# Adding a finished tile's sums to its tokens in two halves, at two places of the next tile

## The chip, the cores and the metric

One core of a Trainium2 chip runs the whole kernel. The metric is the device time of one execution in microseconds (us); lower is better. Engines: PE (TensorE), DVE (VectorE), ACT (ScalarE), POOL (GpSimd), SP (SyncE, which issues loads). On-chip memory is SBUF (the kernel's "arena") and PSUM, eight banks that PE writes.

## The reference, cut to what matters

Two layers of a trunk over 512 latent and 256 context tokens of width 1024. Each has attention, a short and a long convolution, a merge, and then a layer of experts with product keys. The change touches that last part alone:

```python
def chunk(hc):                       # 128 tokens
    q = (hc @ wq).reshape(PEER_CHUNK, PEER_HEADS, 2, PEER_DK // 2)
    s = jnp.einsum('chpd,hpnd->chpn', q, subkeys)
    s1, i1 = lax.top_k(s[:, :, 0], PEER_TOPK)      # 16 of 128
    s2, i2 = lax.top_k(s[:, :, 1], PEER_TOPK)
    ...
    sc, ic = lax.top_k(cand, PEER_TOPK)            # 16 of the 256 sums
    e = ...                                        # expert numbers
    g = jax.nn.softmax(sc, axis=-1)
    a = jax.nn.gelu(jnp.einsum('chkd,cd->chk', u_tab[e], hc))
    return jnp.einsum('chk,chkd->cd', g * a, v_tab[e])
x = x + gt2 * f                                    # f: the chunks' results
```

Each token takes 8 heads x 16 = 128 experts; for each it needs two rows of 1024 numbers, one of `u_tab` and one of `v_tab`. The result of a chunk, times the gate `gt2`, is added to the tokens.

## The kernel before, in words

The class `Experts` works through tiles of 128 tokens: six in the first layer, four in the second. A tile is 8 units (heads) of 16 selections, so 128 selections. For one selection, each of the 128 tokens of the tile has one expert:

- POOL gathers the 128 rows of 2048 numbers (u and v side by side, 1 MB) into one of 8 slots by an indirect DMA (`gather`, L491). It waits for the expert numbers at the start of a unit, and for the slot: `slot_used` must tell that the selection 8 earlier is summed.
- DVE multiplies the u half with the tokens and sums along the row (`dot`, L651): the "dot". It waits for the landing.
- ACT makes the gelu, the weight and a diagonal matrix of it (`weigh`, L504, L508, L515).
- PE multiplies the diagonal with the v half and accumulates in PSUM (`sum_up`, L536). It works in pairs of selections (even, odd): 16 products, of 512 columns each, for a pair, then frees both slots. Even selections put the tokens of each half of the partitions in place, odd ones crosswise.

Two things are put in between on DVE. `dot` steps a generator, `topk`, at k = 3, 5, 7, 9 and 14 of each unit, just after the dot of that k: the five pieces make the 16 experts and the probabilities of the next unit (L549 to L613). And once a tile is summed, its result is added. It lies in four banks of PSUM: half 0 (two banks, 1024 columns) has the products from the upper 64 partitions of the slots, half 1 those from the lower 64. For each half, `add_tile` multiplies two banks with the gates into `junk` (L626) and adds `junk` to the tokens (L629). `junk` is also what the dots write, so all of this is in order on DVE. At the start of a tile, `turn_halves` (L637) makes the crosswise copy of the new tile's tokens for the odd dots.

`add_tile` of a finished tile is called after the second dot of the next one (`SUM_LAG` is 2), or at the end of the last tile. Tiles use the banks in the order (4, 0, 4, 0, 4, 4) in the first layer and (0, 4, 0, 4) in the second (first bank of each). PE waits at the start of a tile for `sum_taken` of the last tile that had the same banks.

The work is spread over phases with barriers. In the first layer a phase with the experts alone (`phase_experts`) goes to 8 dots into the fifth tile (selection 520); the rest of that layer's experts is interleaved with the first stages of the second layer. In the second layer all 512 selections are in one phase of their own. Each phase starts after all engines have finished the one before.

Of the kernel before, what the change touches and what calls it, by code (L numbers as in the profile page):

```python
# [24 lines left out]
ALU = mybir.AluOpType  # L25
# [4 lines left out]
D = 1024  # L30
# [4 lines left out]
NT_LAT, NT_CTX = L_LAT // P, L_CTX // P  # L35
# [363 lines left out]
class Experts:  # L399
# [214 lines left out]
                                ALU.mult).then_inc(self.probs_ready, 1)  # L614
        yield

    def add_tile(self, dve, tile):
        nc, t = self.c.nc, self.tiles[tile]
        x = self.c.xs[:, t]
        dve.wait_ge(self.slot_used, self.per_tile * (tile + 1))  # L620
        dve.wait_ge(self.dotted, self.n_dotted)
        for half in range(2):
            at = self.bank_of(tile, half) * 512
            if half:
                dve.wait_ge(self.x_added, 2 * tile + 1)
            nc.vector.tensor_tensor(self.junk, self.c.psum[:, at:at + D], self.gates[:, t // NT_LAT],  # L626
                                    ALU.mult).then_inc(self.sum_taken, 1)
            dve.wait_ge(self.sum_taken, 2 * tile + half + 1)
            nc.vector.tensor_tensor(x, x, self.junk, ALU.add).then_inc(self.x_added, 1)  # L629
        dve.wait_ge(self.x_added, 2 * tile + 2)  # L630

    def turn_halves(self, dve, tile):
        nc = self.c.nc
# [6 lines left out]
    def dot(self, dve, n):  # L640
        nc = self.c.nc
        for i in range(self.n_dotted, n):
            u, k = divmod(i, TOPK)
            if i % self.per_tile == 0:
                self.turn_halves(dve, i // self.per_tile)
            if k == 0:
                self.parts = self.topk(dve, u + 1) if u + 1 < self.units else iter(())
            if i:
                dve.wait_ge(self.dotted, i)
            dve.wait_ge(self.landed[i % self.ring], 16 * (i // self.ring + 1))  # L650
            nc.vector.scalar_tensor_tensor(out=self.junk, in0=self.slots[i % self.ring][:, 0:D], scalar=1.0,  # L651
                                           in1=self.h2_turned if i % 2 else self.h2N[:, self.tiles[u // PH]],
                                           op0=ALU.mult, op1=ALU.mult, accum_out=self.dots[:, u % 2, k:k + 1]).then_inc(self.dotted, 1)
            self.n_dotted = i + 1
            if k in (3, 5, 7, 9, 14):
                next(self.parts, None)
            tile, j = divmod(self.n_dotted, self.per_tile)
            if tile and j == self.SUM_LAG:
                self.add_tile(dve, tile - 1)
        if n == self.n_all:  # L660
            self.add_tile(dve, len(self.tiles) - 1)


class Share:
# [2175 lines left out]
```

## Time and profile before

| | us |
|---|---|
| median of 3 runs (5434.0 to 5438.31) | 5437.69 |
| profiled execution | 5433.36 |
| its span, first to last instruction | 5431.3 |
| DVE busy | 3330.3 (61%) |
| PE busy | 3760.0 (69%) |
| POOL busy | 2036.3 (37%) |
| ACT busy | 1988.8 (37%) |

The busy shares are means over stages with very different limits; what a change is worth is read from the stage in which it lies. The profile divides the span into 40 slices of 136 us; GB/s is what the DMA engines moved in each. PE's clock can be granted at 2.4 or 1.2 GHz; a granted clock of 0.5 is the lower one, and a mean between 0.5 and 1.0 has both in it.

### The profile page before, as it was taken

The numbers are of one execution on the slowest core, as the hardware profiler recorded it, in microseconds if no ns is written. First come the engines' busy times: TensorE is split into PE (matmuls) and PEld (weight loads), VectorE is DVE, ScalarE is ACT, GpSimd is POOL, SyncE is SP. The second block draws the span as 40 slices with busy tenths as digits, with TensorE's granted clock in tenths as the row PEclk, the third lists the DMA queues.
The fourth block names the chain that finished last, engine by engine and source line by source line (L and its number), as shares of the span: only waits on it lengthen the run. The fifth ranks groups of instructions, "written<-read, shape, count | busy, mean of one in ns | idle before, by whom it ended". The sixth has DMA issues, their size and how long they took to land. (4 is left out here: it accounts for less than half of the span.)

```text
span 5431.3 us, 59703 instructions
## 1 busy us (share of the span) xinstructions
PE 3760.0 (69%) x19504; PEld 1838.0 (34%) x19504; DVE 3330.3 (61%) x7026; ACT 1988.8 (37%) x5136; POOL 2036.3 (37%) x1533
## 2 busy tenths in 40 slices
PE   6899879987565555555577679678976555555554
PEld 3677338876111111111122245246852111111111
DVE  7622452223777777777687777764135777777776
ACT  5432002212443344343354444325223443343443
POOL 5112003212444444444483356211434444444443
PEclk8999989998767777777688889889988777777777
DMA  5012002212999999999998989841327999999998
GB/s 237 16 44 70 4 16 65 63 67 103 400 418 410 416 410 417 415 414 414 378 363 349 367 327 375 349 171 37 98 80 325 421 412 417 413 415 416 411 417 345
DMA packets 230644, 1532.43 MB, mean 282 GB/s; under 512 B 26164, under 2 KB 26740, under 8 KB 58044
## 3 DMA queue, kind: packets, MB, share of 16 engines
q0 software_dynamic: 184320, 1342.26, 60.5%
q1 hardware_dynamic: 46012, 186.36, 9.4%
q8 instruction: 154, 2.52, 0.2%
q14 instruction: 158, 1.29, 0.1%
HBM read 1515.31 MB, written 13.21 MB: 281 GB/s over the span
## 5 line engine op out<-in xcount | busy, mean ns | idle before, releaser
L536 PE MATMUL psum<-arena 64*64 64x512 f32 x10240 | 1769.8, 825 | 1220.8 <-ACT arena L515 1209.6
L491 POOL DMA_INDIRECT arena<-in_uv,arena x1280 | 1462.9, 1143 | 1817.7 <-PE psum L536 1392.6
L651 DVE SCALAR_TENSOR_TENSOR arena<-arena 128x1024 f32<-128x1024 f32 x1280 | 1621.4, 1267 | 697.8 <-DMA arena<-in_uv,arena 653.0
L536 PEld LDWEIGHTS psum<-arena 64*64 64x64 f32 x10240 | 418.1, 169 | 2519.8 <-ACT arena L515 1892.9
L1549 PE MATMUL psum<-view_at,view_at 128*128 128x512 f32 (+1 forms) x4896 | 966.5, 359 | 19.1 <-PEq L165 10.3
L504 ACT ACTIVATE arena<-arena 128x1 f32<-128x1 f32 x1280 | 258.2, 202 | 1850.8 <-DVE arena L651 1811.0
L265 POOL TENSOR_TENSOR view_at<-view_at,view_at 128x1024 fp32r<-128x1024 f32 (+1 forms) x192 | 455.2, 2380 | 1238.7 <-ACT view_at L299 1208.4
L1549 PEld LDWEIGHTS psum<-view_at,view_at 128*128 128x128 f32 x4896 | 815.3, 191 | 185.2 <-issue 54.4
L515 ACT ACTIVATE arena<-arena 128x64 f32<-128x64 f32 x1280 | 445.1, 348 | 52.7 <-PE psum L536 10.9
L508 ACT ACTIVATE arena<-arena 128x1 f32<-128x1 f32 x1280 | 376.9, 294 | 46.7 <-ACT arena L504 0.4
L299 ACT ACTIVATE view_at<-view_at 128x1024 fp32r<-128x1024 f32 (+1 forms) x176 | 163.9, 939 | 330.6 <-DMA view_at<-in_w_in 188.2
L2405 DVE TENSOR_TENSOR view_at<-view_at,psum 128x768 f32<-128x768 f32 (+1 forms) x48 | 39.4, 821 | 376.2 <-PE psum L1549 376.2
L265 DVE TENSOR_TENSOR view_at<-view_at,view_at 128x2048 fp32r<-128x2048 f32 (+5 forms) x106 | 177.0, 1697 | 83.7 <-ACT view_at L2371 37.2
L2468 PE MATMUL psum<-view_at,view_at 128*128 128x512 f32 x480 | 114.5, 402 | 35.2 <-DVE view_at L265 34.1
L1269 PE MATMUL psum<-view_at,view_at 128*128 128x256 f32 (+1 forms) x528 | 96.7, 346 | 28.1 <-PEq L165 28.1
L2468 PEld LDWEIGHTS psum<-view_at,view_at 128*128 128x128 f32 x480 | 93.4, 195 | 56.0 <-issue 34.6
L504 ACT ACT_TABLE_LOAD x85 | 109.1, 1283 | 2.9 <-PEq L165 1.4
L1019 PE MATMUL psum<-view_at,cond 128*4 128x512 f32 x192 | 63.0, 466 | 64.8 <-POOL view_at L265 35.7
L651 DVE DVE_READ_ACCUMULATOR arena<-arena 128x1 f32 x1280 | 104.8, 82 | 0.0
L2240 PE MATMUL psum<-arena 128*128 128x256 f32 (+2 forms) x232 | 80.0, 511 | 34.6 <-DVE arena L2282 34.6
L558 DVE MAX8 arena<-arena 128x8 f32<-128x128 f32 (+1 forms) x240 | 81.5, 339 | 35.9 <-DVE arena L556 1.5
L472 ACT ACT_TABLE_LOAD x80 | 102.6, 1283 | 1.4
(246 smaller groups left out, 3445.6 us busy)
## 6 DMA issues: line engine op xcount, KB each, us to landing
view_at<-in_w_in SPq DMA_DIRECT2D x108, 512.0 KB, 6.6
view_at<-in_w_mod SPq DMA_DIRECT2D x48, 1024.0 KB, 12.9
arena<-in_uv,arena POOLq DMA_INDIRECT x1280
view_at<-in_w_br SPq DMA_DIRECT2D x48, 256.0 KB
view_at<-in_w_out SPq DMA_DIRECT2D x16, 512.0 KB, 8.7
view_at<-in_wq SPq DMA_DIRECT2D x16, 512.0 KB, 3.4
arena<-mod_rows SPq DMA_DIRECT2D x12, 512.0 KB
keep_spectrum<-arena SPq DMA_DIRECT2D x18, 256.0 KB, 6.9
```

The source lines that it names most:

```text
L265: return eng.tensor_tensor(lo, x, hi.bitcast(F32), ALU.subtract)
L299: self._high(act, lambda out, x: self.c.nc.scalar.activation(out, x, ACT.Copy), n)
L472: self.c.nc.scalar.activation(self.exps[:, u % 2], self.topc, ACT.Exp, bias=self.small[:, u % 2, 0:1], accum_out=self.small[:, u % 2, 1:2] ...
L491: nc.gpsimd.indirect_dma_start(out=self.slots[i % self.ring], out_offset=None, in_=self.table, in_offset=bass.IndirectOffsetOnAxis(ap=self ...
L504: nc.scalar.activation(self.gelus[:, q, k:k + 1], self.dots[:, q, k:k + 1], ACT.Gelu).then_inc(self.act_steps, 1)
L508: nc.scalar.activation(self.scaled[:, q, k:k + 1], self.gelus[:, q, k:k + 1], ACT.Copy, scale=self.probs[:, q, k:k + 1]).then_inc(self.act ...
L515: nc.scalar.activation(self.diag[:, i % 4], self.ident2, ACT.Copy, scale=self.scaled[:, q, k:k + 1]).then_inc(self.diag_ready, 1)
L536: last = nc.tensor.matmul(self.c.psum[tokens, at:at + 512], self.diag[rows, k % 4], self.slots[k % self.ring][rows, D + h * 512:D + (h + 1 ...
L651: nc.vector.scalar_tensor_tensor(out=self.junk, in0=self.slots[i % self.ring][:, 0:D], scalar=1.0, in1=self.h2_turned if i % 2 else self.h ...
L1269: last = nc.tensor.matmul(out, h[:, k, at], m[:, lo:hi, k, :], start=(k == 0 and i == 0), stop=(k == KD - 1 and i == 2))
L1549: last = nc.tensor.matmul(c.psum[:, at + lo:at + hi], a[:, k], b[:, k, lo:hi], start=(k == 0 and i == 0), stop=(k == kt - 1 and i == 2))
L2468: last = nc.tensor.matmul(c.bank(2 * (t % 4) + h), a[:, k, t * P:(t + 1) * P], b[:, 4 * h:4 * h + 4, k, :], start=(k == 0 and i == 0), sto ...
```

## The change

The addition of a finished tile is split into its two halves. Where the next tile uses other banks, the first half is added after 5 dots of it and the second after 7; where it uses the same banks, both are added after 2 dots, as before. The last tile of a layer is added at its end, as before.

```diff
-    def add_tile(self, dve, tile):
+    def add_half(self, dve, tile, half):
         nc, t = self.c.nc, self.tiles[tile]
-        x = self.c.xs[:, t]
+        x, at = self.c.xs[:, t], self.bank_of(tile, half) * 512
         dve.wait_ge(self.slot_used, self.per_tile * (tile + 1))
         dve.wait_ge(self.dotted, self.n_dotted)
-        for half in range(2):
-            at = self.bank_of(tile, half) * 512
-            if half:
-                dve.wait_ge(self.x_added, 2 * tile + 1)
-            nc.vector.tensor_tensor(self.junk, self.c.psum[:, at:at + D], self.gates[:, t // NT_LAT],
-                                    ALU.mult).then_inc(self.sum_taken, 1)
-            dve.wait_ge(self.sum_taken, 2 * tile + half + 1)
-            nc.vector.tensor_tensor(x, x, self.junk, ALU.add).then_inc(self.x_added, 1)
-        dve.wait_ge(self.x_added, 2 * tile + 2)
+        if half:
+            dve.wait_ge(self.x_added, 2 * tile + 1)
+        nc.vector.tensor_tensor(self.junk, self.c.psum[:, at:at + D], self.gates[:, t // NT_LAT],
+                                ALU.mult).then_inc(self.sum_taken, 1)
+        dve.wait_ge(self.sum_taken, 2 * tile + half + 1)
+        nc.vector.tensor_tensor(x, x, self.junk, ALU.add).then_inc(self.x_added, 1)
+        dve.wait_ge(self.x_added, 2 * tile + half + 1)
+
+    def add_after(self, tile):
+        same = tile + 1 < len(self.tiles) and self.banks[tile + 1] == self.banks[tile]
+        return (self.SUM_LAG, self.SUM_LAG) if same else (5, 7)
...
             tile, j = divmod(self.n_dotted, self.per_tile)
-            if tile and j == self.SUM_LAG:
-                self.add_tile(dve, tile - 1)
+            for half in range(2):
+                if tile and tile < len(self.tiles) and j == self.add_after(tile - 1)[half]:
+                    self.add_half(dve, tile - 1, half)
         if n == self.n_all:
-            self.add_tile(dve, len(self.tiles) - 1)
+            for half in range(2):
+                self.add_half(dve, len(self.tiles) - 1, half)
```

## Rows read from the trace of the kernel before

**Rows 1.** The page: span; GB/s in 40 slices; the group of the dots.
```profile
span 5431.3 us, 59703 instructions
...
GB/s 237 16 44 70 4 16 65 63 67 103 400 418 410 416 410 417 415 414 414 378 363 349 367 327 375 349 171 37 98 80 325 421 412 417 413 415 416 411 417 345
...
L651 DVE SCALAR_TENSOR_TENSOR arena<-arena 128x1024 f32<-128x1024 f32 x1280 | 1621.4, 1267 | 697.8 <-DMA arena<-in_uv,arena 653.0
```

**Rows 2.** The copies of L637: durations (ns), first and last start.
```profile
L637 DVE COPY arena<-arena x20: 686/689/691, 1354.1 to 5083.8; 64x1024 f32<-64x1024 f32 x20
```

**Rows 3.** Timeline of DVE, undisturbed: start, duration, idle before; eight dots, first and last.
```profile
5385.25 1.22 DVE L651 SCALAR_TENSOR_TENSOR arena<-arena 128x1024 f32<-128x1024 f32 x1 [1.25 <-DMA arena<-in_uv,arena]
...
5402.64 1.23 DVE L651 SCALAR_TENSOR_TENSOR arena<-arena 128x1024 f32<-128x1024 f32 x1 [1.25 <-DMA arena<-in_uv,arena]
```

**Rows 4.** Timeline of DVE, second tile of the second layer: turn, dots 1 to 13.
```profile
4433.52 1.41 DVE L637 COPY arena<-arena 64x1024 f32<-64x1024 f32 x2
...
4437.22 1.23 DVE L651 SCALAR_TENSOR_TENSOR arena<-arena 128x1024 f32<-128x1024 f32 x1 [1.03 <-DMA arena<-in_uv,arena]
...
4438.56 1.22 DVE L626 TENSOR_TENSOR arena<-psum,arena 128x1024 f32<-128x1024 f32 x1
...
4443.59 1.22 DVE L651 SCALAR_TENSOR_TENSOR arena<-arena 128x1024 f32<-128x1024 f32 x1
...
4444.86 1.22 DVE L651 SCALAR_TENSOR_TENSOR arena<-arena 128x1024 f32<-128x1024 f32 x1
...
4448.04 1.23 DVE L651 SCALAR_TENSOR_TENSOR arena<-arena 128x1024 f32<-128x1024 f32 x1
...
4453.76 1.22 DVE L651 SCALAR_TENSOR_TENSOR arena<-arena 128x1024 f32<-128x1024 f32 x1
...
4458.29 1.23 DVE L651 SCALAR_TENSOR_TENSOR arena<-arena 128x1024 f32<-128x1024 f32 x1
...
4459.56 1.22 DVE L651 SCALAR_TENSOR_TENSOR arena<-arena 128x1024 f32<-128x1024 f32 x1
...
4463.95 1.22 DVE L651 SCALAR_TENSOR_TENSOR arena<-arena 128x1024 f32<-128x1024 f32 x1
...
4468.57 1.23 DVE L651 SCALAR_TENSOR_TENSOR arena<-arena 128x1024 f32<-128x1024 f32 x1 [0.85 <-DMA arena<-in_uv,arena]
```

**Rows 5.** Timeline of POOL in the same stretch: gathers of selections 10 and 14.
```profile
4451.62 0.94 POOL L491 DMA_INDIRECT arena<-in_uv,arena  x1 [5.99 <-PE psum L536]
...
4458.78 1.56 POOL L491 DMA_INDIRECT arena<-in_uv,arena  x1 [1.74 <-PE psum L536]
```

**Rows 6.** Timeline of PE in the same stretch: products of two pairs.
```profile
4447.09 3.69 PE L536 MATMUL psum<-arena 64*64 64x512 f32 x16 [5.20 <-ACT arena L515]
4451.54 1.95 PE L536 MATMUL psum<-arena 64*64 64x512 f32 x16 [0.76 <-ACT arena L515]
```

**Rows 7.** Windows: busy us of each engine, granted clock, DMA share, GB/s (last).
```profile
4435.00:4465.00 30.00, 14.66 (x96) 3.41 (x88) 26.80 (x62) 8.45 (x30) 15.36 (x12) 0.77 0.99 392
...
4465.00:4759.70 294.70, 170.40 (x936) 39.73 (x936) 213.33 (x530) 122.89 (x386) 127.92 (x116) 0.72 1.01 415
...
4454.00:4460.00 6.00, 1.95 (x16) 0.51 (x16) 5.35 (x15) 1.89 (x7) 3.65 (x4) 1.00 0.89 306
```

**Rows 8.** Timeline at the end of the first layer's pure stage.
```profile
2672.01 0.15 DVE L578 TENSOR_SCALAR arena<-arena 128x1 f32<-128x1 f32 x1
2672.87 0.33 SPq L954 DMA_DIRECT2D cols<-in_cols  x1
```

**Rows 9.** Timeline: a gather of POOL and the dot of the same selection.
```profile
4676.18 0.94 POOL L491 DMA_INDIRECT arena<-in_uv,arena  x1 [5.34 <-issue]
...
4683.68 1.23 DVE L651 SCALAR_TENSOR_TENSOR arena<-arena 128x1024 f32<-128x1024 f32 x1 [1.29 <-DMA arena<-in_uv,arena]
```

**Rows 10.** Timeline of POOL, then a window: the first gather of the first layer.
```profile
1336.04 1.17 POOL L491 DMA_INDIRECT arena<-in_uv,arena  x1 [4.00 <-DVE arena L601]
...
1337.00:1338.00 1.00, 0.79 (x15) 0.60 (x14) 0.00 (x0) 0.38 (x1) 0.70 (x2) 1.00 0.37 66
```

## The prediction

> **What bounds the kernel now.** I read the page first. The change touches only the expert stage, in which 1280 selections are gathered (1 MB each), dotted with their tokens (L651) and summed. In the slices that hold this stage alone (two stretches of some 1300 us) the core moves 400 to 421 GB/s [rows 1], and nearly all of DVE's idle time before its dots is put down to the landing of a gather. So the stage goes at the pace of its transfers. When nothing disturbs it, a dot starts every 2.485 us: seven steps in 17.39 us [rows 3]. A dot itself takes 1.27 us, so DVE has 1.2 us to spare in each. What DVE does besides costs nothing until it makes DVE so late that the gathers behind it are held up.
>
> How a late dot comes to hold up a transfer: there are eight slots, and the gather of selection m+7 goes into the slot of m-1, which is free once PE has summed the pair (m-1, m). PE waits for ACT's weight, and ACT for the dot of m. Hence the question for every extra microsecond on DVE: how far behind the landings is the *odd* dot of a pair, and how long before its due landing is the next gather issued?
>
> **The transition before.** The timeline of DVE shows one in full [rows 4]. I count selections of the new tile from 0. Dot 1 starts at 4437.22, on waiting for its data; the four operations of the addition run from 4438.56 to 4443.59 (5.03 us), with no wait for PE before them. With dot 1 as time 0, selection j lands at 2.485 (j-1). Dots 2 to 10 start at 6.4, 7.6, 10.8, 12.1, 15.3, 16.5, 21.1, 22.3 and 26.7: the second dot of a pair follows after 1.27, and the pieces of top-k behind dots 3 and 5 take the step to 3.18 us (4444.86 to 4448.04), behind 7 to 4.53, behind 9 to 4.39 [rows 4]. So the lags behind the landings are 3.9, 2.7, 3.4, 2.1, 2.8, 1.6, 3.7, 2.5 and 4.4. DVE has caught up at 4468.57 (dot 13). From dot 1 to there 12 selections took 31.35 us, where 29.82 were due: 1.5 us lost. Not all of that is the addition's: the same transfers lose about as much in places without any addition, since a whole tile lasts 324.8 us, where 128 x 2.485 = 318.1 were due (two tiles lie between the turn at 4433.5 [rows 4] and that of the last tile, whose second copy starts at 5083.8 [rows 2] and the first 0.7 earlier). The windows separate the two better. The 30 us from the start of the tile move 392 GB/s, the other 294.7 us of the tile 415 [rows 7]; over the six full transitions it is 392 to 416, 401 in the mean, against 415. So an addition costs (1 - 401/415) x 30 = 1.0 us of transfer at the most. **This is all that there is to win: six times 1.0 = 6 us, 0.1% of the span.**
>
> **The change part by part.**
>
> *Counts.* Eight tiles are followed by another. In the one case with the same banks (first layer, tile 4 to 5) both halves still come at 2, and the two last tiles of the layers are added as before. Seven transitions change: six inside the pure stage, and tile 3 to 4 of the first layer, which lies right before the end of its phase.
>
> *Instructions.* The same four operations of DVE per tile, none more. The waits on slots and on the last dot are issued twice; before, the first pair of them costs 0.1 us between the end of dot 1 (4437.22 + 1.23) and the addition (4438.56). I take 0.1 us of DVE more per transition, beneath what the rows resolve. The waits on PE are met later than before and were already met then, so they stay free. PE's wait for free banks comes a tile later and is met either way. SP and ACT get nothing new; no DMA issue is added or moved on POOL, but each stands behind the dot that frees its slot.
>
> *Where the work falls.* This is the point. At 2 the addition meets a DVE that is on time, and it has two dots to recover in before top-k starts. At 5 and 7 each half (2.5 us; with its dot the step is 1.34 + 2.52 = 3.86) falls between pieces of top-k, and inside a pair: the first dot of the pair is done, the second, which PE needs, is held back. I run the same recurrence: a dot starts at its landing or when DVE is free. Dots 2 to 11 start at 2.5, 5.0, 8.2, 12.0, 15.2, 19.1, 23.6, 24.9, 29.2 and 30.5, and the lags are 0, 0, 0.7, 2.1, 2.8, 4.1, 6.2, 5.0, 6.9 and 5.7. The odd ones are what counts: before 2.7, 2.1, 1.6, 2.5, 3.2 (dots 3, 5, 7, 9, 11), after 0, 2.1, 4.1, 5.0, 5.7. The change trades one early, modest delay for a later and greater one: from dot 7 on everything is 2.5 us later than before.
>
> *What that does to the gathers.* From the start of an odd dot to the issue of the gather that it frees, the trace has 6.76 us (4444.86 to 4451.62), and 5.02 where PE is quick (4453.76 to 4458.78) [rows 4, 5]. The difference is PE's: 3.69 us for the 16 products of a pair at the granted clock of 1.2 GHz after 5.20 us of idleness, 1.95 at 2.4 GHz [rows 6]. The due landing is 7 x 2.485 = 17.4 us after that of the odd dot. The margin from issue to due landing is thus 17.4 - lag - (5.0 to 6.8). Before, the narrowest is 17.4 - 2.7 - 6.8 = 7.9 us, behind dot 3, and 2 us later the rate falls to 306 GB/s for 6 us [rows 7]. After, it is 6.5 to 8.3 behind dot 7, 5.6 to 7.4 behind 9 and 4.9 to 6.7 behind 11; the slow figures are likelier, since PE now idles 5 us before each of these pairs.
>
> *Its price.* The trace shows no gather with so short a margin in full flow. Upper bound: one issued at 4676.18 was there for its dot at 4683.68, 7.50 us later, and DVE had idled 1.29 us before it, as in the undisturbed beat (1.25) [rows 3, 9]; so 7.5 costs next to nothing; if nothing shorter did, the narrowest margin of 4.9 would cost 2.6 us. Lower bound: the first gather of the stage is issued at 1336.04, and its data begin to move within 2 us (66 GB/s between 1337 and 1338) [rows 10]; with 2.5 us of moving that makes 4.5, less than 4.9, and the loss would be nothing. The middle of the likely margins, 5.5, lies one microsecond above the lower end and two below the upper; I take 0.9. Against it stands what is saved at dot 3, between 0 and 1.0 us; since half of the dip there falls away only to come back later, I take 0.4. Net per transition +0.5 us, from -1.0 to +2.6; six of them **+3.0**.
>
> The Trainium skill ("DMA: Bandwidth & Descriptors", on the anatomy of a gpsimd DMA) gives a DMA issued by gpsimd 2.0 us plus its bytes at 436 GB/s; for 1 MB this is an estimate of 4.4 us. By that rule even the narrowest margin suffices and only the saving is left, so that the six would give -2.4 where my sum has +3.0. The rows here neither confirm nor exclude it, as none that they show goes below 7.5 us.
>
> *The end of the phase.* In the first layer the pure stage ends after 8 dots of tile 4. DVE ends it: its last piece of top-k starts at 2672.01 and the next phase's first load is issued at 2672.87 [rows 8]. That piece stands behind dot 7, which is 2.5 us later after the change (19.1 against 16.5). Every engine meets at this barrier, so nothing hides it: **+2.5**, at least 0 if the next phase's first loads were not what it waits for.
>
> *Sum.* 3.0 + 2.5 = +5.5 us. The profiled execution took 5433.4 us (span 5431.3), which makes 5438.9; against the median of the runs, 5437.7, which lies 4.3 above it, **5443.2 us**.
>
> **The rivals.** A measurement of this kernel tells about 0.2%, 10.9 us, from no change.
> (a) *The ring runs dry* (slower). Each late gather costs the whole upper price: the place is the gathers issued behind dots 7, 9 and 11; 6 x 2.6 + 2.5 = +18.1, 5455.8 us. It decides from (10.9 - 2.5)/6 = 1.4 us net per transition. For it: the narrowest margin falls from 7.9 to as little as 4.9 us, at three gathers in a row, and PE stays at its lower clock. Against it: even 4.9 covers the start and the moving of the first gather's rows [rows 10].
> (b) *The ring holds, and the dip is gone* (a little faster). Six times -1.0, + 2.5 = -3.5, 5434.2 us. For it: the lower bound of the price, and that the early dip has its cause removed. Against it: the later lags are twice the earlier. The rule of the Trainium skill named above points to this case. Still within 0.2%: faster by over 0.2% would need 13 us from the transitions, where only 6 are lost.
> (c) *The change does nothing to the stage*: as DVE is on time again by dot 15, only the barrier moves: +2.5, 5440.2.
>
> **How the numbers follow.** My forecast 0.45, (c) 0.22, (b) 0.17, (a) 0.16. The likeliest is 5443.2. The range reaches from (b) to a little short of (a)'s end: 5434 to 5455. Slower by over 0.2% is (a) less its weaker part, plus a little of the forecast's upper tail: 0.15. Faster by over 0.2%, for something that no row shows: 0.03. Within 0.2%: 0.82.
>
> **What would show it.** In the timeline of DVE around a transition: two operations behind dot 4, two behind dot 6, no wait for PE; dots 2 and 3 on waiting for their data; dot 10 about 29 us after dot 1. On POOL: the gap of 7 us before the gather of selection 10 gone, longer gaps before 14, 16 and 18. In the windows: the dip of transfer moved by some 10 us to later and not smaller. At the end of the first pure phase: the last piece of top-k 2.5 us later relative to the tile's start. I am wrong if the rate in the 45 us behind a transition falls by more than 1.4 us of transfer (a), or if the pace has no dip at all (b).

## The result, and the profile after

The changed kernel takes 5445.63 us (median of 21 runs, 5437.76 to 5452.53), the kernel before in the same 21 rounds 5435.33 (5428.42 to 5443.33). The ratio is 1.0018, 95% interval 1.0012 to 1.0024: slower by some 10 us (6.5 to 13), where I had forecast +5.5 and put the time at 5443.2, range 5434 to 5455. So the forecast held in direction and range, but the loss is nearly twice my sum. The interval lies on both sides of 0.2%, and the estimate itself is below it. In the rounds of the experiments, one execution of e8 (6048.5 us) and one of the kernel before (5561.7) ran at a lower mean granted clock (0.62 and 0.72, where the others have 0.81 to 0.82), and the ratios leave them out. The profiled execution has a span of 5443.3 us against 5431.3; single executions of either kernel differ by 10 us and more, so what follows goes by stretches of the trace and not by spans.

The timeline of DVE at the same place of the changed kernel as [rows 4] (start, duration, kind of operation, idle before). The lines of the dots are now L655, of the addition L625 and L628. The rows are dots 1, 4, the first half, 5, 6, the second half, 7, 8, 10, 13, 19, 20 and 21:

```profile
4444.98 1.23 DVE L655 SCALAR_TENSOR_TENSOR arena<-arena 128x1024 f32<-128x1024 f32 x1 [0.98 <-DMA arena<-in_uv,arena]
...
4453.71 1.22 DVE L655 SCALAR_TENSOR_TENSOR arena<-arena 128x1024 f32<-128x1024 f32 x1
...
4455.05 1.23 DVE L625 TENSOR_TENSOR arena<-psum,arena 128x1024 f32<-128x1024 f32 x1
...
4457.57 1.22 DVE L655 SCALAR_TENSOR_TENSOR arena<-arena 128x1024 f32<-128x1024 f32 x1
...
4460.76 1.22 DVE L655 SCALAR_TENSOR_TENSOR arena<-arena 128x1024 f32<-128x1024 f32 x1
...
4462.09 1.22 DVE L625 TENSOR_TENSOR arena<-psum,arena 128x1024 f32<-128x1024 f32 x1
...
4464.60 1.22 DVE L655 SCALAR_TENSOR_TENSOR arena<-arena 128x1024 f32<-128x1024 f32 x1
...
4469.11 1.23 DVE L655 SCALAR_TENSOR_TENSOR arena<-arena 128x1024 f32<-128x1024 f32 x1
...
4474.77 1.23 DVE L655 SCALAR_TENSOR_TENSOR arena<-arena 128x1024 f32<-128x1024 f32 x1
...
4478.57 1.22 DVE L655 SCALAR_TENSOR_TENSOR arena<-arena 128x1024 f32<-128x1024 f32 x1
...
4492.41 1.22 DVE L655 SCALAR_TENSOR_TENSOR arena<-arena 128x1024 f32<-128x1024 f32 x1 [1.35 <-DMA arena<-in_uv,arena]
...
4496.69 1.23 DVE L655 SCALAR_TENSOR_TENSOR arena<-arena 128x1024 f32<-128x1024 f32 x1 [1.12 <-DMA arena<-in_uv,arena]
...
4499.10 1.23 DVE L655 SCALAR_TENSOR_TENSOR arena<-arena 128x1024 f32<-128x1024 f32 x1 [1.18 <-DMA arena<-in_uv,arena]
```

From dot 4 on DVE runs without a pause: dots 5, 6, 7, 8 and 10 come 3.9, 7.1, 10.9, 15.4 and 21.1 us after dot 4, and the recurrence of the prediction said 3.8, 7.0, 10.9, 15.4 and 21.0. (Dot 4 itself is 8.7 us after dot 1 here and not 8.2, because the data of dot 2 came 0.6 us late; in the other five transitions it is 8.1 or 8.2.) Neither half waits for PE. What I had not foreseen is further down: from dot 19 to dot 21, two selections, 6.69 us pass where 4.97 are due.

The step is lost at dot 20: it waits 1.12 us for its data, behind the piece of top-k that dot 19 brings. POOL and ACT show why. The gather of selection 20 goes into the slot of selection 12, which the pair (12, 13) frees. The rows of POOL are the gathers of selections 10, 14, 18 and 20:

```profile
4457.24 1.11 POOL L491 DMA_INDIRECT arena<-in_uv,arena  x1 [4.64 <-PE psum L536]
...
4471.12 1.30 POOL L491 DMA_INDIRECT arena<-in_uv,arena  x1 [4.48 <-PE psum L536]
...
4482.80 1.45 POOL L491 DMA_INDIRECT arena<-in_uv,arena  x1 [3.46 <-PE psum L536]
...
4487.97 1.43 POOL L491 DMA_INDIRECT arena<-in_uv,arena  x1 [2.48 <-PE psum L536]
```

Dot 20 starts 8.72 us after the start of its gather (4487.97 to 4496.69). And ACT between the weights of selections 12 and 13, from the end of the one (the L515 that starts at 4479.13) to the start of the other (the L504 of 4482.51):

```profile
4479.13 0.35 ACT L515 ACTIVATE arena<-arena 128x64 f32<-128x64 f32 x1
4479.50 1.28 ACT L472 ACT_TABLE_LOAD   x1
4480.79 0.31 ACT L472 ACTIVATE arena<-arena 128x16 f32<-128x16 f32 x1
4481.01 0.19 ACT L472 ACTIVATION_READ_ACCUMULATOR arena<-arena 128x1 f32 x1
4481.21 1.28 ACT L504 ACT_TABLE_LOAD   x1
4482.51 0.20 ACT L504 ACTIVATE arena<-arena 128x1 f32<-128x1 f32 x1
```

ACT makes the exponential of the next unit after selection 12, with a table load before it and one back to the gelu, 3.0 us in all. The weight of 13 stands behind it. So from dot 13 to the gather that its pair frees it is 9.4 us here (4478.57 to 4487.97), and not 5.0 to 6.8 as behind the odd dots before it. (The Trainium skill, "ScalarE: Activation LUTs", on what a table load costs, gives 1283 ns for the load and some 1380 ns more for a drain; the load agrees with the row's 1.28, the drain does not show: the exponential starts 1.29 us after the start of its load.) The kernel before has the same wait (8.3 us in the mean of the six transitions, 8.6 after), but there DVE is 1.0 us behind the beat at dot 13, and after the change 3.3.

The prediction also named signs on POOL. The gap before the gather of selection 10 (5.6 us in the mean of the six transitions; I had written 7, and the row has 5.99) falls to 2.2 and is not gone. The gaps before 12 and 14 grow (0.8 to 5.5 and 1.7 to 4.7), those before 16 and 18 do not (3.9 to 3.1 and 3.5 to 3.1), against what I had written of 16 and 18.

The windows: busy us of the engines, granted clock, DMA share and GB/s (last). First the kernel before, then the changed one, each the 55 us from dot 0 of the tile of [rows 4] and the 263 us behind them; for the changed kernel then four shorter stretches, which show the dip:

```profile
4435.00:4490.00 55.00, 29.64 (x176) 7.08 (x168) 43.23 (x98) 20.87 (x69) 26.48 (x23) 0.75 1.00 405
...
4490.00:4753.00 263.00, 150.82 (x832) 34.83 (x832) 191.82 (x481) 106.10 (x336) 113.99 (x104) 0.72 1.00 415
```

```profile
4442.80:4497.80 55.00, 31.44 (x176) 7.43 (x168) 41.51 (x94) 19.66 (x64) 25.24 (x22) 0.75 0.98 377
...
4497.80:4760.80 263.00, 149.45 (x824) 34.08 (x824) 192.29 (x484) 105.13 (x336) 117.58 (x104) 0.72 1.01 417
...
4443.00:4463.00 20.00, 10.24 (x64) 2.42 (x56) 14.71 (x33) 5.92 (x21) 9.56 (x8) 0.83 0.99 392
4463.00:4473.00 10.00, 4.17 (x24) 1.01 (x24) 9.21 (x24) 2.54 (x9) 3.72 (x4) 0.83 0.96 400
4473.00:4483.00 10.00, 6.36 (x32) 1.22 (x24) 9.40 (x22) 5.96 (x15) 3.58 (x4) 0.51 0.96 332
4483.00:4493.00 10.00, 7.31 (x48) 1.98 (x48) 4.73 (x9) 4.39 (x17) 6.30 (x6) 0.80 0.97 377
```

The dip has moved from 19 to 25 us after dot 0 [rows 7] to 30 to 50 us, and it is longer. Over the six transitions the 55 us move 409, 405, 404, 405, 411, 401 GB/s before (mean 406) and 388, 381, 387, 377, 395, 376 after (mean 384). At 416 GB/s that is (406 - 384)/416 x 55 = 2.9 us of transfer less. But in the five stretches of 263 us behind them it is 415 to 417 before (mean 416.2) and 417 to 420 after (mean 418.2), which gives 1.3 us back. So each transition loses 1.6 us net by the bytes; by the tiles' lengths, below, 0.8 to 1.3. The bytes of a stretch are a rough measure: e3, the kernel with the shortest tiles below, moves only 397 GB/s in its first 55 us and 418.8 behind them.

The prediction had set a sign of being wrong: more than 1.4 us of transfer less in the 45 us behind a transition, which was to speak for rival (a). These 45 us move 402.7 GB/s before and 385.5 after (means of six), 1.9 us of transfer less. So this sign was met. The rival is still not borne out, since its price of 2.6 us a transition is twice what the tiles show; the sign was set on a stretch that ends before a part of the loss has come back.

The end of the first layer's pure stage, in the changed kernel: dots 0 and 7 of the fifth tile, the last piece of top-k, the next phase's first load. It answers to [rows 8]:

```profile
2650.95 1.23 DVE L655 SCALAR_TENSOR_TENSOR arena<-arena 128x1024 f32<-128x1024 f32 x1
...
2672.57 1.23 DVE L655 SCALAR_TENSOR_TENSOR arena<-arena 128x1024 f32<-128x1024 f32 x1
...
2676.99 0.15 DVE L578 TENSOR_SCALAR arena<-arena 128x1 f32<-128x1 f32 x1
...
2677.85 0.33 SPq L960 DMA_DIRECT2D cols<-in_cols  x1
```

From dot 0 to dot 7 it is 21.6 us; before, 19.1. Again DVE ends the phase, 0.86 us ahead of the first load, as it did [rows 8].

### The profile page after: what moved, and what is told of

It is laid out like the page before. It is cut to its first block and busy times, and to the rows that moved or that the text cites. A ratio compares the mean times of both kernels' runs of the same rounds, so it can differ in the third digit from the quotient of the medians.

```text
span 5443.3 us, 59716 instructions
## 1 busy us (share of the span) xinstructions
PE 3737.6 (69%) x19504; PEld 1830.2 (34%) x19504; DVE 3337.2 (61%) x7026; ACT 1988.9 (37%) x5136; POOL 2014.9 (37%) x1533
## 3 DMA queue, kind: packets, MB, share of 16 engines
q14 instruction: 158, 1.29, 0.1%
## 5 line engine op out<-in xcount | busy, mean ns | idle before, releaser
L491 POOL DMA_INDIRECT arena<-in_uv,arena x1280 | 1439.7, 1125 | 1846.2 <-PE psum L536 1405.5
L655 DVE SCALAR_TENSOR_TENSOR arena<-arena 128x1024 f32<-128x1024 f32 x1280 | 1625.1, 1270 | 701.7 <-DMA arena<-in_uv,arena 655.1
L504 ACT ACTIVATE arena<-arena 128x1 f32<-128x1 f32 x1280 | 258.0, 202 | 1854.3 <-DVE arena L655 1785.1
L515 ACT ACTIVATE arena<-arena 128x64 f32<-128x64 f32 x1280 | 445.1, 348 | 57.1 <-PE psum L536 15.3
L504 ACT ACT_TABLE_LOAD x85 | 109.1, 1283 | 2.9 <-PEq L165 1.4
L655 DVE DVE_READ_ACCUMULATOR arena<-arena 128x1 f32 x1280 | 105.2, 82 | 0.0
L472 ACT ACT_TABLE_LOAD x80 | 102.6, 1283 | 1.4
```

Of the source, the lines that this page charges most:

```text
L472: self.c.nc.scalar.activation(self.exps[:, u % 2], self.topc, ACT.Exp, bias=self.small[:, u % 2, 0:1], accum_out=self.small[:, u % 2, 1:2] ...
L491: nc.gpsimd.indirect_dma_start(out=self.slots[i % self.ring], out_offset=None, in_=self.table, in_offset=bass.IndirectOffsetOnAxis(ap=self ...
L504: nc.scalar.activation(self.gelus[:, q, k:k + 1], self.dots[:, q, k:k + 1], ACT.Gelu).then_inc(self.act_steps, 1)
L515: nc.scalar.activation(self.diag[:, i % 4], self.ident2, ACT.Copy, scale=self.scaled[:, q, k:k + 1]).then_inc(self.diag_ready, 1)
```

## The experiments

Two lengths are read from the timeline of DVE in each profile. **Six tiles**: the six inner tiles that follow a transition in the pure stages, from the first dot of the tile to the first of the next (the last one, which the end of the stage cuts, to its dot 116), added up. **Eight dots**: from dot 0 to dot 7 at the end of the first layer's pure stage. I also give **lost by dot 21**: how much later than its due time of 2.485 us per selection dot 21 starts, counted from dot 1, mean of the six transitions. Medians of a run are compared with those of the kernel before in the same rounds.

| | halves after | six tiles | eight dots | lost by dot 21 | ratio to before (95%) |
|---|---|---|---|---|---|
| before | 2, 2 | 1916.7 | 19.1 | 1.3 | |
| the change | 5, 7 | 1924.5 | 21.6 | 3.3 | 1.0018 (1.0012 to 1.0024) |
| e1_2_4 | 2, 4 | 1915.2 | 19.1 | 1.2 | 0.9998 (0.9989 to 1.0007) |
| e2_4_6 | 4, 6 | 1921.4 | 21.1 | 3.4 | 1.0011 (1.0002 to 1.0020) |
| e3_12_28 | 12, 28; end 2, 2 | 1914.0 | 19.0 | 1.3 | 0.9993 (0.9984 to 1.0002) |
| e4_5_7_not_end | 5, 7; end 2, 2 | 1921.6 | 19.0 | 3.2 | 1.0009 (1.0000 to 1.0018) |
| e5_exp9_5_7 | 5, 7; exponential after 9 | 1921.3 | 21.6 | 2.5 | 1.0015 (1.0006 to 1.0024) |
| e6_exp9_before | 2, 2; exponential after 9 | 1915.1 | 19.1 | 1.2 | 1.0001 (0.9992 to 1.0010) |
| e7_exp9_12_28 | 12, 28; end 2, 2; exponential after 9 | 1914.9 | 19.0 | 0.9 | 1.0000 (0.9991 to 1.0009) |
| e8_9_9 | 9, 9; end 2, 2 | 1923.5 | 19.2 | 3.8 | 1.0018 (1.0009 to 1.0026) |
| e9_split_2_2 | 2, 2, as two calls | 1915.2 | 19.2 | 1.1 | 1.0003 (0.9994 to 1.0011) |
| e10_only_end | 2, 2; end 5, 7 | 1916.0 | 21.3 | 1.3 | 1.0004 (0.9996 to 1.0013) |
| e11_seven_slots_before | 2, 2; seven slots | 1955.3 | 20.5 | 3.9 | 1.0140 (1.0123 to 1.0158) |
| e12_seven_slots_5_7 | 5, 7; seven slots | 1975.8 | 23.5 | 6.1 | 1.0163 (1.0142 to 1.0184) |

The lengths come from one profile of each kernel. The seven kernels with eight slots and no late addition in the six tiles (before, e1, e3, e6, e7, e9, e10) lie between 1914.0 and 1916.7; this is how well the six tiles can be read. The five with one (the change, e2, e4, e5, e8) lie between 1921.3 and 1924.5. The means are 1915.3 and 1922.5, 7.2 us apart, or 1.2 us a transition. The total is known to 0.1% only, 3 to 5 us, so that the finer questions hang on the stretches.

The edits of e1 to e4 and e8 to e10 are in the return of `add_after` alone, and e7 has one there besides. END and REST stand here for the two pairs of numbers:

```diff
-        return (self.SUM_LAG, self.SUM_LAG) if same else (5, 7)
+        if len(self.tiles) == NT and tile == NT_LAT - 1:
+            return END
+        return (self.SUM_LAG, self.SUM_LAG) if same else REST
```

### Does the place inside a pair matter, or the splitting? (e1, e2, e9)

END and REST are (2, 4), (4, 6) and (2, 2).

> The halves come after 2 and 4 dots everywhere (3 tokens tiles of each layer and the end of the phase alike). Theory L (lateness: what counts is how far behind its landing the second dot of each pair starts, wherever the addition stands): the recurrence gives lags of 0.2, 2.1, 1.6, 2.5 and 3.2 us for dots 3, 5, 7, 9, 11, against 2.7, 2.1, 1.6, 2.5, 3.2 before, so the early dip goes and nothing comes later; the six inner tiles last 0 to 1 us less each than before, the end of the phase is unchanged, total 0 to -6 us against before. Rival S (splitting the addition, with its repeated waits, costs in itself): the six tiles last about 1.3 us longer each, as with the change, total some +8.

> The halves come after 4 and 6 dots, so between pairs, not inside them. Theory L: the first dots of the pairs are later than with the change, the second ones as late (2.0, 4.0, 4.9, 5.6 us for dots 5, 7, 9, 11 against 2.1, 4.1, 5.0, 5.7), so it costs what the change costs: six tiles about 1.3 us longer than before each, barrier 2.4 us later, total +10. Rival P (the loss comes from holding a pair open after its first dot): the inner tiles are as long as before, total +2.5.

> The code of the change with both halves after 2 dots everywhere, so only the repeated waits are new. Theory L: like before within 2 us, six tiles 1915 to 1918 us, eight dots at the end of the phase 19.1 us from first to last. Rival S (splitting costs in itself): longer in the six tiles, up to the 1922 to 1925 us of the change.

Splitting costs nothing: e9 and e1 are at 1915.2, with the kernels that are not split. The place within a pair doesn't matter either: with both halves between pairs (e2) the six tiles take 1921.4, the eight dots 21.1, and dot 21 has lost 3.4 us, near the change or e4 in all three (rival P had 1916 and a total of +2.5). What it does depend on is when the second dot of a pair starts, as lateness (theory L) has it. In e1 the early lag at dot 3 is gone and nothing comes later, and the six tiles are 1.5 us below before in all: the early dip, which the aggregate rate shows [rows 7], was worth 0 to 0.3 us a tile, not resolved from nothing (e9, which has that dip, is at 1915.2 too).

### Out of the way of top-k (e3)

END (2, 2), REST (12, 28).

> The halves come after 12 dots of the first and of the second unit of the next tile, where top-k leaves DVE alone; at the end of the pure stage of the first layer both come at 2 as before. Theory L: no lag above those of a unit without any addition but 1.6 us at dot 13, which has recovered two dots later; the dips of the transitions vanish, each of the six tiles up to 1 us shorter than before, total 0 to -6 us. Rival S: longer by some 1.3 us a tile. If the early dip was no loss at all, the total is that of before.

Six tiles 1914.0, the lowest of all, total 0.9993 (0.9984 to 1.0002): at the favourable place there is little or nothing to win, as the bound of the prediction (6 us) said. No version in this study is measurably faster than the kernel before.

### The end of the phase alone, and all but it (e4, e10)

END (2, 2), REST (5, 7), and the reverse.

> The change, except that the addition of the fourth tile of the first layer, just before the phase ends, stays at 2. Theory L: the eight dots at the end of that phase take 19.1 us from the first to the last as before and not 21.6, so the total is 2.5 us less than with the change, +7 to +8 against before; the six inner tiles as long as with the change (together 8 us longer than before). Rival B (most of the change's cost comes through the barrier and what starts after it): close to before, +2 or less.

> The change only at the end of the first layer's pure stage (5 and 7 there, 2 and 2 elsewhere). Theory L: the eight dots take 21.6 us and not 19.1, the six tiles 1915 to 1918 us as before, total +2.5 us. If the phase behind the barrier hides the delay, the total is that of before and the stretch from there to the second layer's experts is 2.5 us shorter.

The two parts come apart in the stretches as expected: e4 has the long tiles (1921.6) and the short end (19.0), e10 the short tiles (1916.0) and the long end (21.3). Whether the next phase hides the delay stays open. From dot 7 to the first dot of the second layer it is 1449.0 us before, 1450.3 in e10 and 1452.0 in the changed kernel, and 1448.0 and 1448.1 in e2 and e5, which have the late end too. But among the kernels with eight slots and the early end the stretch runs from 1448.0 (e1) to 1453.9 (e8), so 2.5 us given back there would not be seen. The totals, +0.9 and +0.4 thousandths, add up to 1.3 where the change has 1.8, all within their intervals; that of e10 (-0.4 to +1.3) has both +2.5 us and nothing in it. Rival B (the barrier carries most) is not borne out: the six tiles of e4 are 5 us above before.

### The gather behind dot 13 (e5, e6, e7)

In the loop of `weigh`, for the change, the kernel before and e3:

```diff
-            if k == 12 and u + 1 < self.units:
+            if k == 9 and u + 1 < self.units:
                 self.softmax_exp(act, u + 1)
```

> The change as it is, but ACT makes the next unit's exponential after selection 9 of each unit, while DVE is busy with the fourth piece of top-k, and not after selection 12. Theory A (part of the change's cost is the gather behind dot 13: ACT puts 3.1 us of two table loads and the exponential between the weights of selections 12 and 13, so its slot comes free 8.6 us after the dot and not 5 to 6.8): that wait falls to below 7 us, the step lost between dots 19 and 21 of each transition (0.8 us against 0.1 before) goes, six inner tiles 3 to 6 us shorter in all than with the change, total +3 to +7 against before. Rival D (all of the cost comes from the gathers behind dots 7, 9 and 11, and 13 only inherits it): the same lateness shows up one pair later, six tiles as with the change (1921 to 1925 us), total +8 to +10.

> The kernel before, with the exponential after selection 9. Theory A: without the late additions the gather behind dot 13 has 8 to 9 us of margin and loses nothing, so the total is that of before within 2 us either way; the wait from dot 13 to its gather falls from 8.3 us to below 7. If it is clearly faster (over 5 us), the table loads cost something in every unit and not in the transitions alone.

> Halves after 12 and 28 dots (2 and 2 at the end of the phase) together with the exponential after selection 9. Theory L with A: every odd dot has a margin of over 8 us; six tiles at or below the 1914 us of the kernel with 12 and 28 alone, total 2 to 6 us below before. If the margin never was what loses time before, it equals before.

In e5 the way from dot 13 to the gather that its pair frees is 6.9 us in the mean of the six transitions (8.6 with the change), and the step of dots 19 to 21 loses nothing more: lost by dot 19 and by dot 21 are 2.4 and 2.5 us, with the change 2.5 and 3.3. The same place as above, DVE of e5, dots 13, 19 and 21 (the last is 5.00 us after 19; it was 6.69), then on POOL the gather of selection 20, which now stands right behind the two before it:

```profile
4474.29 1.22 DVE L655 SCALAR_TENSOR_TENSOR arena<-arena 128x1024 f32<-128x1024 f32 x1
...
4488.62 1.22 DVE L655 SCALAR_TENSOR_TENSOR arena<-arena 128x1024 f32<-128x1024 f32 x1 [1.24 <-DMA arena<-in_uv,arena]
...
4493.62 1.22 DVE L655 SCALAR_TENSOR_TENSOR arena<-arena 128x1024 f32<-128x1024 f32 x1 [0.58 <-DMA arena<-in_uv,arena]
```

```profile
4481.79 1.54 POOL L491 DMA_INDIRECT arena<-in_uv,arena  x1 [0.30 <-issue]
```

So up to dot 21 the gather behind dot 13 costs 0.6 to 0.8 us of each transition (e4 and the change), and theory A holds for the place. It does not hold for the length. The six tiles of e5 take 1921.3, against 1924.5 and 1921.6 in the two profiles with the late halves and the old exponential (the change and e4), so this wait is worth at most 3 us in all and perhaps nothing. Followed further, e4 and e5 are 4.2 and 3.3 us behind at dot 25, but both 4.3 at dot 61: what e5 had saved is gone by then. And e2, whose wait behind dot 13 is 8.9 us, loses only 0.3 between dots 19 and 21, since it is 3.1 late at dot 19 already. The total of +8 us (1.0015) and the tiles lie where rival D had put them, though not for its reason, since the lateness doesn't come back one pair later. That all of the cost lies in the gathers behind dots 7, 9 and 11 is thus not excluded for the tile as a whole. Without late additions the same edit changes nothing (e6, 1.0001; e7, 1.0000), although the wait falls there too (8.3 us to 6.9 in e6, 9.4 in e3 to 6.6 in e7): a wait that had margin is worth nothing when it shrinks. For e7 I had expected 2 to 6 us less than before, which did not come.

### More lateness (e8)

END (2, 2), REST (9, 9).

> A stronger dose of lateness: both halves after 9 dots (at the end of the phase after 2, as before). The recurrence gives lags of 5.9, 6.6 and 4.2 us for dots 9, 11 and 13 against 5.0, 5.7 and 3.2 with the change, so margins one microsecond narrower. Theory L: one microsecond more is lost per transition, six tiles 4 to 6 us longer than with the change (1926 to 1930 us), without the barrier's 2.5 us, total +10 to +14 against before. A theory by which lateness costs a fixed amount once the ring is behind: six tiles as with the change, total +7.

By dot 21 the transitions have lost 3.8 us, 0.5 more than with the change. The six tiles take 1923.5, no more than with it. The total, 1.0018 (1.0009 to 1.0026) or +10, is at the lower end of what theory L gave, and its interval has the +7 of the fixed amount in it. My proportional price is thus not borne out: of a loss at the transition only a part is left at the end of the tile. The windows of the changed kernel show the same, more GB/s than before in the 263 us behind the dip.

### One slot fewer (e11, e12)

```diff
-        self.slots = [c.at(24 + 8 * i, 2 * D) for i in range(7)] + [c.at(104, 2 * D)]
+        self.slots = [c.at(24 + 8 * i, 2 * D) for i in range(7)]
```

> The kernel before with seven slots instead of eight, so every gather is issued 2.49 us nearer to its due landing. Theory L: margins behind dots 3, 11 and 13 fall from 8 to between 5 and 6 us, and a usual unit, without any addition, has 6.6 us behind dot 13; the transitions lose about what the change loses with eight slots (1 to 2 us each), usual units little, total +8 to +30 against before. A theory in which the number of free slots doesn't matter: no difference.

> The change with seven slots. Theory L: margins behind dots 7, 9, 11 and 13 fall to between 2.4 and 4.3 us, less than any gather needs (5.3 at least in the runs so far), so that each transition loses 1 to 2.5 us more than the change loses with eight: 10 to 20 us above the kernel before with seven slots, where the difference with eight is 10. A theory in which lateness costs a fixed amount: 8 to 10 us above it, as with eight slots.

The seventh slot alone carries +77.8 us (5511.29 against 5433.48), much above the expected 8 to 30: usual units lose too. The first tile of the first layer, which no addition precedes, takes 328.4 us and not 319.1. The change on top of it costs 5529.11 - 5511.29 = 17.8 us by the medians of four runs each, and 12.5 by the ratios, whose intervals overlap; so the total does not separate the expected 10 to 20 from a fixed 8 to 10. The stretches speak for more than the fixed amount: the six tiles differ by 20.5 us (0.5 to 6.9 a tile, where with eight slots it is 0.8 to 2.1), the eight dots by 3.0. But it comes in another place than I had expected. By dot 21 the change has lost 2.2 us more than the kernel before, as with eight slots (2.1). With eight slots 0.7 of this comes back by the end of the tile; with seven it grows to 2.8. So the slots that are left decide what becomes of a loss, by one profile of each kernel. (The 5.3 us of the expectation is not in the timelines: from issue to the start of its dot no gather took less than 5.9 us in the runs before this round, and the shortest in e12 took 5.36.) A gather that landed in time, in the kernel with seven slots and the old places, POOL and then the dot of the same selection, 5.52 us later:

```profile
1932.72 0.95 POOL L491 DMA_INDIRECT arena<-in_uv,arena  x1 [3.59 <-PE psum L536]
...
1938.24 1.22 DVE L651 SCALAR_TENSOR_TENSOR arena<-arena 128x1024 f32<-128x1024 f32 x1 [1.26 <-DMA arena<-in_uv,arena]
```

## Why the prediction was right, and where it was off

*What bounds the stage, and how lateness reaches the transfers*: shown. From dot 4 on the starts of the dots came out as the recurrence gave them, to 0.1 us; the place inside a pair and the splitting don't matter (e1, e2, e9); the number of slots does (e11, 78 us).

*"This is all that there is to win: six times 1.0 = 6 us"*: held as a bound. At the best place (e3) the six tiles are 2.7 us shorter than in the profile of before, and 1.2 shorter than in e9, which adds at the same place as before. The saving of 0.4 us per transition, which I set against the cost, was too high: e1, which keeps just this saving, gains 1.5 us in six tiles against before and nothing against e9, and by dot 21 it has gained 0.1.

*The end of the phase, +2.5*: 19.1 to 21.6 us, right for the phase itself, and again alone in e10 (21.3). That nothing behind the barrier hides it was argued; the runs do not resolve it.

*The price of a transition, +0.5 net, +3.0 in all*: this term was mis-sized. The six tiles grew by 7.8 us in the profile of the change and by 4.9 in e4, so 0.8 to 1.3 us each; with the 2.5 of the barrier that makes +7.4 to +10.3, and +10 was measured. Two parts of the term were off. The saving of 0.4 was at most 0.3 and perhaps nothing, as above. And the price of 0.9, a value chosen between 4.5 us, which was to cost nothing, and 7.5, was too low: e5 with the shortened wait behind dot 13 and e6, which has that wait shortened too but no late halves, differ by 1.3 us at dot 21 and by 1.0 us a tile (1921.3 against 1915.1), and that is what the gathers behind dots 7, 9 and 11 cost net of the saving.

One step of the sum was also wrong in itself, the one that reads "The margin from issue to due landing is thus 17.4 - lag - (5.0 to 6.8)" and names the gathers behind dots 7, 9 and 11 as the narrow ones. Behind dot 13 the term in brackets is 8.6 us, by ACT's table loads, which the trace of before would have shown (8.3 there). With a lag of 3.3 the margin is 5.5 us, as narrow as behind 9 and 11 (5.8 and 5.3, by the mean waits of 6.6 and 6.4). Up to dot 21 this gather loses 0.6 to 0.8 us more per transition; at the end of the tile no loss from it is resolved (e4 against e5). So it explains the lost step at dot 20 and not, as far as is known, the excess of the total. That the forecast fell on the right side of its range owes something to the width of that range: the term for the six transitions was +3.0, and 4.9 to 7.8 was measured. It is luck, too, that the forecast time misses by only 2.4 us where the forecast loss misses by 5: it was put on a median of three runs, 5437.7, and the 21 runs of the kernel before have 5435.3.

*The upper and lower price*: 2.6 us a transition (rival a) and nothing (rivals b and c) are both excluded by the six tiles. The rule of the Trainium skill ("DMA: Bandwidth & Descriptors", anatomy of a gpsimd DMA) by which 4.4 us suffice would have given -2.4 for the six: it doesn't hold for a gather behind others. The gather of selection 20 above took 8.72 us to a dot that waited for it, and one of the shortest, in the kernel with seven slots, 5.52 us. With the change data come late behind dots 9, 11 and 13, at mean margins of 5.8, 5.3 and 5.5 us; behind dot 7 (6.6) DVE itself is so late that the rows can't tell. Since the time from issue to landing varies this much, no single margin separates in time from late; the prediction's two bounds were each one gather.

*Open*: why a part of the loss comes back within the tile (e8 in place of a proportional loss; 418.2 GB/s against 416.2 behind the dip). A gather counts as landed when its semaphore has been raised 16 times, and the traces show how far apart these 16 are. For selection 14 of a tile, first to last, it is 2.2 to 3.8 us before and 1.3 to 2.6 behind the dip of the changed kernel; for selection 60, 3.7 to 4.5 and 2.5 to 3.6; for selection 80, 3.4 to 4.4 and 3.0 to 4.6. So the parts of a transfer come closer together behind a pause and drift apart again within the tile. That would bring landings forward for a while and fits the part that comes back, but no experiment changed it by itself, so as a cause it is argued, not shown. Open too is whether the phase behind the barrier takes back any of the 2.5 us.

## What to carry to other kernels

In a stage that goes at the pace of its transfers through a ring of slots, ask of every operation that is moved how late it makes the consumer that *frees* the slot, and run the recurrence over a whole period: work put ahead of other bursts is recovered before they come, work put among them adds to them. The way from consumer to freed slot isn't one number: walk it for each position of the period, through each engine on the way, since one position may have a wait (here two table loads) that only shows once the margin is gone. And follow a loss to the end of its stretch before it is priced: here a loss of 2.1 us at dot 21 was 0.8 to 1.3 us at the end of the tile. Count, too, what the move does at the end of the phase: the phase itself ends later by all of it (2.5 us here), and what the work behind the barrier makes of that has to be measured.

## What the runs showed that I had not expected

One slot of eight is worth 78 us (1.4%), some eight times what the change costs, though with eight slots the kernel seems not to want for any. And the time lost behind a dip in the transfers is partly made good with eight slots (a mean of 2.9 us of transfer fewer in the first 55 us of a tile, 1.3 us more in the next 263), and with seven it is not.
